# Issuing the page copies of the cached keys and values after the fourth product of the first projection

## The reference

```python
u = rmsnorm(x, norm1_g)
z = u @ w_in + b_in                      # one projection for both mixers and the merge gates
h_m = mlstm(z, state_conv, state_C, state_n, state_m)
h_n = nsa(z, cache_kv[page_table], cache_win_kv)
h = x + merge(z, h_m, h_n)
y = rmsnorm(h + moe(rmsnorm(h)), normf_g)   # 32 experts, 4 for each token
```

## Time and profile before

| | |
|---|---|
| median of 3 runs | 1607.19 us (1605.06 to 1610.12) |
| profiled execution | 1603.71 us |
| its span, first to last instruction | 1602.1 us |
| mean granted TensorE clock | 0.989 |

### The profile page before, as it was taken

One profiled execution on the slowest core, in us unless ns is written; L12 is line 12 of the kernel. 1 busy time (PEld: TensorE's weight loads), 2 busy tenths in 40 slices (PEclk: granted clock), 3 DMA queues, 4 the chain that ended last, 5 costly groups with the idle time before them and its releaser, 6 DMA issues.

```text
span 1602.1 us, 22042 instructions
## 1 busy us (share of the span) xinstructions
PE 1509.5 (94%) x8565; PEld 710.9 (44%) x8565; DVE 545.5 (34%) x1184; ACT 316.6 (20%) x711; POOL 53.0 (3%) x121
## 2 busy tenths in 40 slices
PE   8999998999988999999999999999999999999996
PEld 5447555666865675333333333333333333333332
DVE  4511333344455332532323232332232322322323
ACT  2301221244335400311111111111111111111112
POOL 5410000000000000000000000000000000000000
PEclk9999999899999999999999999999999999999998
DMA  9933356152454496599999999999999999999995
GB/s 339 395 123 106 121 181 132 54 168 119 145 158 158 111 306 273 207 368 426 425 428 428 427 428 429 427 428 428 427 428 428 427 428 428 427 429 427 427 429 221
DMA packets 99713, 507.33 MB, mean 317 GB/s; under 512 B 19127, under 2 KB 57387, under 8 KB 73897
## 3 DMA queue, kind: packets, MB, share of 16 engines
q1 hardware_dynamic: 95522, 482.78, 75.8%
q0 software_dynamic: 4080, 23.73, 3.9%
q10 hardware_dynamic: 54, 0.05, 0.0%
HBM read 499.38 MB, written 28.06 MB: 329 GB/s over the span
## 4 chain that ended last, share of the span: by engine, by line
PE 33%; DMA 29%; DVE 3%; issue 1%; ACT 0%; DVEq 0%; SPq 0%
DMA wring<-w_gu 25%; PE bank L2117 14%; PE bank L2158 8%; DMA zf<-w_gu 4%; PE bank L1969 4%; PE bank L1978 2%; PE bank L2059 1%; PE bank L1954 1%; DVE zf L2490 1%; DVE zf L2488 1%; DVE zf L2486 1%; PE bank L1987 0%; PE bank L1950 0%; PE bank L2092 0%; PE bank L2086 0%
## 5 line engine op out<-in xcount | busy, mean ns | idle before, releaser
L2117 PE MATMUL bank<-wring,zf 128*64 128x512 f32 x1600 | 360.5, 596 | 25.2 <-DMA wring<-w_gu 24.8
L2117 PEld LDWEIGHTS bank<-wring,zf 128*64 128x64 f32 x1600 | 108.8, 136 | 250.4 <-issue 192.4
L2470 DVE SCALAR_TENSOR_TENSOR x<-bank,wt,x 128x512 f32<-128x512 f32 x155 | 104.9, 744 | 196.5 <-PE bank L2059 196.5
L2158 PE MATMUL bank<-wring,zf 128*64 128x512 f32 x768 | 170.1, 595 | 0.7
L2201 ACT ACTIVATE zf<-bank 128x512 f32<-128x512 f32 (+1 forms) x133 | 75.8, 594 | 316.1 <-PE bank L2158 214.8
L2117 PE MATMUL bank<-zf 128*64 128x512 f32 x448 | 100.8, 596 | 6.2 <-DMA zf<-w_gu 6.2
L2476 DVE TENSOR_TENSOR zf<-bank,zf 128x512 f32<-128x512 f32 x32 | 22.1, 692 | 224.5 <-ACT zf L2201 224.5
L2158 PEld LDWEIGHTS bank<-wring,zf 128*64 128x64 f32 x768 | 53.3, 137 | 98.9 <-issue 97.0
L954 PE MATMUL bank<-uT,w_slots 128*128 128x320 f32 x256 | 80.3, 462 | 1.2 <-ACT zf L1087 1.2
L1969 PE MATMUL bank<-zf,wring 128*128 128x320 f32 x256 | 69.1, 433 | 0.9 <-PEq L1279 0.9
L2059 PE MATMUL bank<-zf,eqw 64*128 64x512 bf16 x558 | 69.3, 380 | 0.0
(11 more groups left out here) (528 smaller groups left out, 1686.6 us busy)
## 6 DMA issues: line engine op xcount, KB each, us to landing
wring<-w_gu SPq DMA_DIRECT2D x100, 2048.0 KB, 32.6
wring<-w_dn SPq DMA_DIRECT2D x48, 2048.0 KB, 34.5
zf<-w_gu SPq DMA_DIRECT2D x28, 2048.0 KB, 32.8
zf<-w_dn SPq DMA_DIRECT2D x16, 2048.0 KB, 34.3
w_slots<-w_in SPq DMA_DIRECT2D x11, 2048.0 KB, 9.1
kv_linear<-cache_kv POOLq DMA_DIRECT2D x64, 256.0 KB, 5.3
kv_stage<-kv_linear SPq DMA_DIRECT2D x16, 1024.0 KB, 9.2
w_slots<-w_in SPq DMA_DIRECT2D x4, 1024.0 KB, 7.8
```

Source lines behind the costliest of these rows:

```text
L2117: last = pe.matmul(half(2 + gu, h), xe[:, k % 4, k // 4, :], m.ring[slot(k // 2)][:, o:o + H], start=False, stop=(k == KD - 1))
L2158: last = pe.matmul(half(4, h), atT[:, k % 4, k // 4, :], m.ring[slot(4 + k // 4)][:, o:o + H], start=(k == 0), stop=(k == 7))
L2470: dve.scalar_tensor_tensor(part(r), m.bank[SCATTER_BANKS[r]][:, :], wt[:, r // 2, bass.ds(i - 1, 1)], part(r), ALU.mult, ALU.add).then_inc ...
```

## The change

One line is added to POOL's list, between its wait for the page table and the loop that issues the 64 page copies. POOL now also waits until the fourth product of the first projection is done, the same count at which SP issues chunk 2. Nothing is removed, and the order of each engine's list stays as it was.

```diff
             pool.wait_ge(s_pages, 16)
+            pool.wait_ge(s_pd, 4)
             for b in range(NB):
                 for j in range(NPG):
                     page = pool.value_load(...)
                     pool.dma_start(m.kv_lin[b, j], a.cache_kv[...]...).then_inc(s_lin, 16)
```

## The result

| | before | changed |
|---|---|---|
| first comparison, median of 8 and 8 runs | 1607.16 us (1602.25 to 1612.55) | 1599.98 us (1596.33 to 1601.67) |
| ratio, 95% interval | | 0.9948 [0.9931, 0.9965] |
| second comparison, another chip | 1604.9 us, 34 runs | 1600.16 us, 12 runs, ratio 0.9982 [0.9958, 1.0006] |
| third comparison, another chip | 1606.32 us, 23 runs | 1598.9 us, 10 runs, ratio 0.9964 [0.9948, 0.9980] |
| profiled execution (span) | 1603.71 us (1602.1) | 1596.75 us (1595.1) |

What follows compares the result with a forecast made beforehand. TensorE was taken to set the pace until an unbroken expert-weight DMA stream bounds the end. Removing a 3.14 us wait and 1.70 us of half clock gives 1607.19 - 4.84 = 1602.4 us, range 1599.5 to 1607.2.

Steps and rivals of the forecast that it cites:

- What bounds the kernel, and where the change acts: TensorE sets the pace until the expert-weight stream; time saved in the first stage should reach the end in full.
- The wait goes: Behind the gate products: chunk 2 lands at 53 to 57 us, before TensorE wants it at 61.28, saving 3.14 us.
- The half clock goes: First L401 product, behind the wait: without idle time the clock stays at 1.00, saving 1.70 us, bounds 0 and 1.70.
- The size of the saving: Front of the kernel: 3.14 + 1.70 = 4.84 us less, everything after shifted as it is.
- Landings beside the copies: Weight chunks loaded while page copies run: 13.1 to 17.1 us from issue to landing, 15 taken for chunk 2.
- the 18 that the prediction named as a sign of being wrong: Any weight chunk taking over 18 us to land would show the forecast wrong.
- POOL's order: POOL's queue: copies from about 40.3 to 111.8 us, the outputs queued behind them delayed at no cost, first memory at 160.3.
- (a): Rival behind the gate products: the clock falls anyway, owed to their narrow work; gain 3.14 us alone, 1604.0; chance 0.09.
- (b): Rival at chunks 2, 3 and 4: engines alternate packets, a chunk gets a fifth of the rate; slower, 1618; chance 0.06.
- (c): Rival at chunk 4: it lands late by up to 3 us; 1603 to 1607; chance 0.07.
- (d): Rival at chunk 2: held by SP's own backlog, not the copies, so nothing moves; 1607.2; chance 0.06.
- First expert weights near 581 us: Start of the expert-weight stream: SP issues its first load near 581 us, before at 585.76, a sign of being right.

Runs made afterwards that it cites:

- e5: Changed kernel with the copies waiting for the first product instead of the fourth, 13 us earlier; ratio 0.9967 [0.9946, 0.9988].
- e9: Kernel before, copies from 12 us on as there, but SP's two loads of state_C issued behind chunk 2; ratio 0.9964 [0.9943, 0.9984].
- e7: Kernel before with the gate products done twice; traced wait for chunk 2 1.56 us, 24.27 us from the gate products to L406.
- e11: Kernel before without edit, its fourth trace; wait for chunk 2 2.06 us, 20.46 us from the gate products to the first L405.
- e6: Changed kernel with the copies waiting for the twelfth token-major product, 89 us later; ratio 1.0089 [1.0059, 1.0119].
- e2: Changed kernel without edit, run again beside the kernel before; ratio 0.9982 [0.9958, 1.0006].
- e10: Changed kernel without edit, run a third time; ratio 0.9964 [0.9948, 0.9980].
- e12: Kernel before without edit, its fifth trace; wait for chunk 2 2.64 us, 22.75 us from the gate products to the first L405.
- e8: Kernel before without edit, its third trace; wait for chunk 2 6.18 us, 26.47 us from the gate products to the first L405.

## Why the prediction was wrong, point by point

**What bounds the kernel, and where the change acts: right.** The wait for chunk 2 was the only one that the change touches, and the stages behind it keep their lengths but for the clock. That the saving is carried to the end in full was wrong in the traces (below).

**The wait goes: right, and for the reason given.** SP's queue has moved 9.74 MB by 39.6 us in place of 7.95, and in e5 the same 9.74 MB, so nothing of its earlier loads is left; e5 and e9 show the backlog from both sides.

**The half clock goes: right.** Granted clock 1.00 from 56.8 to 67.8 us, and e7 and e11 show that narrow work without a longer idle stretch does not bring it.

**The size of the saving, and what was made of it: this is the step that failed.** The sum took 3.14 + 1.70 = 4.84 us from one execution as if it were a constant, and let it reach the end whole, "everything after shifted as it is". I gave it no scatter of its own and put the whole effect on the border of what can be told from no change, so that "within 0.3%" came out the likeliest case (0.51). Measured were 7.2 us between the medians of the first comparison (0.52% by the ratio, 0.35% at the near end of its interval) and 0.35% on average of three. In place of the constant the five traces have 2.1 to 8.1 us, 5.0 on average: as a centre 4.84 was near, but by luck of the trace. In place of the whole shift the traces give back 4.6 us from the end of the front on, in stages with more half clock. The time of 1599.98 us lies in the range given, 2.4 us below the forecast. Why the first comparison shows 7.2 us and not 4.84 stays open. A part of it may be the draw: its runs of before have a median of 1607.16 where 84 runs have 1605.5, and over all runs the difference is 5.7 us, between 3.7 and 6.9, which includes 4.84.

**Landings beside the copies: the bounds were too narrow on both sides.** Forecast 13 to 17 us; chunk 2 takes 9.8, 10.4 and 9.8 in the three traces, since the first copy is issued 1.6 us after it and the copies build up slowly (1.34 MB of them between 40 and 50 us, against 1.84 in e5, where chunk 2 took 14.4); chunk 3 takes 16.9, 19.5 and 17.3; chunk 4, the tight one, 16.5, 15.1 and 13.2, in time within its 18.2. The 19.5 is over the 18 that the prediction named as a sign of being wrong, but chunk 3 had 22.8 us: no wait came of it.

**POOL's order: right.** Copies from 41.71 to 113.20 (forecast 40.3 to 111.8), the first memory at 160.65 (160.3). e6 shows that this cover ends, though not where.

**The rivals.** (a) is out by e7. (b), the copies taking four fifths of the engines, did not happen: in e5 each queue had half the bytes, with four of the chunk's packets to one of the copies'. The section of the Trainium skill cited there ("DMA: Bandwidth & Descriptors", section "Queues, rings and completion order") lets an engine drain a whole packet, typically about 9 to 17 descriptors, before it changes queues. It doesn't say how such a packet relates to one of the profile's; the prediction took them for the same, and with 886 packets beside 226 the trace doesn't agree with turns of one profile packet each. (c) did not happen. (d) did not happen, but had a part in it: e9 removes the wait by shortening SP's list with the copies in place, so the wait needs both SP's list and the copies.

**First expert weights near 581 us: right in one trace of three, by luck.** They are issued at 581.07 in the first trace, where 1.2 us were lost at the end of the front but the half-clock stretch at 518 us was missing; in e2 and e10 at 585.24 and 587.82. The five traces of before have 582.01 to 590.19, 585.9 on average, so the three of the changed kernel are only 1.2 us earlier on average. That is the sign the prediction itself had named as wrong, the saving lost again between 130 and 586 us.

**What stays open.** The five traced executions of before have a mean of 1602.1 us and the three of the changed kernel 1600.6, 1.5 us apart; the medians of all runs are 5.7 us apart. The five of before alone lie up to 8 us from each other, so eight executions are too few to decide between the two. That the wait goes and the front gains 5.0 us is shown, and so is the half clock that takes most of it back in the traces. What makes up the 5.7 us of the timed runs, longer waits or less half clock in runs that were not traced, is not shown.

## What to carry to other kernels

A wait for a transfer at the end of a full queue varies with the backlog of that execution: read it from several traces before taking it for a constant. A saving in an early stage need not reach the end: follow it from stage to stage in several traces, with the granted clock beside it. Transfers that nobody reads for 200 us belong behind those that somebody reads in 20, but only until they stand in front of the next load on their own issuing queue: of four later places for the copies, three gave the same gain and the fourth cost 13 us. An idle stretch on TensorE is charged twice when the clock falls with it, here 1.70 us on top of 3.14.

## What the runs showed of the hardware

- Two queues that both had work shared the DMA engines nearly evenly by bytes, not by packets: 1.81 and 1.84 MB in 10 us in e5, at 886 and 226 packets; in the first trace of before, between 53.2 and 70 us, 3.10 and 3.83 MB at 1530 and 473.
- Behind the gate products an idle stretch of 2.06 us on TensorE left the clock at full speed (e11), as did 1.56 us (e7); with 2.64 us (e12), 3.14, 3.76 and 6.18 us the clock fell to half, in e8 while TensorE still stood idle.
- The clock also fell while TensorE was busy: at 253.2 us in the changed kernel, 2.15 us into a row of 64 by 64 transposes that had 0.80 us of idle time ahead of it.
